# SSD's and mLSTM's output norms moved out of the stage behind RWKV into the scans, and five more products of zeros in each chunk of the scan

## The reference, cut to what matters

```python
def _group_norm(y, g, n_groups, center, eps=1e-5):
    yf = y.reshape(shp[:-1] + (n_groups, shp[-1] // n_groups))
    if center:
        yf = yf - jnp.mean(yf, axis=-1, keepdims=True)
    yf = yf * lax.rsqrt(jnp.mean(yf * yf, axis=-1, keepdims=True) + eps)
    return yf.reshape(shp) * g
# SSD:   _group_norm((y_f + y_b + d_skip * xs) * silu(z), norm_g, 2, center=False)
# RWKV:  _group_norm(o_f + o_b, norm_g, 4, center=True) * gate
# mLSTM: _group_norm(h_f + h_b, norm_g, 4, center=True) * sigmoid(o)
y = concat([y_ssd, y_rwkv, y_ml]) @ w_out;  x = x + g1 * y
```

## Time and profile before

| | us |
|---|---|
| median of 3 runs | 2280.27 |
| the runs | 2279.90, 2280.27, 2293.11 |
| the profiled execution | 2292.93 |
| its span, first to last instruction | 2291.2 |
| PE busy in it | 2125.0 (93%) |
| DVE, ACT, POOL busy | 838.0, 773.7, 742.2 |

### The profile page before, as it was taken

One profiled execution on the slowest core, in us unless ns is written; L12 is line 12 of the kernel. 1 busy time (PEld: TensorE's weight loads), 2 busy tenths in 40 slices (PEclk: granted clock), 3 DMA queues, 4 the chain that ended last, 5 costly groups with the idle time before them and its releaser, 6 DMA issues.

```text
span 2291.2 us, 46135 instructions
## 1 busy us (share of the span) xinstructions
PE 2125.0 (93%) x20582; PEld 1973.0 (86%) x20590; DVE 838.0 (37%) x1385; ACT 773.7 (34%) x1369; POOL 742.2 (32%) x543
## 2 busy tenths in 40 slices
PE   6999999889789999999979989988878899999999
PEld 6998766778589999999979987677868899999998
DVE  5845265464650111011148453655455311110112
ACT  4535453333242222121154364433232422222212
POOL 6432261224123333333322222522242233333331
PEclk8999998999899999999989999999998899999999
DMA  7553101000012222234326431010001122222222
GB/s 251 177 157 114 51 8 38 5 3 3 27 49 74 76 80 75 74 117 143 92 83 193 130 115 30 1 39 5 3 2 47 56 74 74 74 77 78 68 76 72
DMA packets 254305, 166.67 MB, mean 73 GB/s; under 512 B 23746, under 2 KB 228036, under 8 KB 254108
## 3 DMA queue, kind: packets, MB, share of 16 engines
q1 hardware_dynamic: 253881, 163.66, 24.1%
q10 hardware_dynamic: 227, 0.07, 0.0%
HBM read 159.59 MB, written 4.12 MB: 71 GB/s over the span
## 4 chain that ended last, share of the span: by engine, by line
PE 84%; DVE 6%; ACT 5%; issue 2%; POOL 1%; SPq 1%; DMA 0%; another core or an unknown queue 0%; DVEq 0%; ACTq 0%; POOLq 0%
PE PS L979 21%; PE PS L981 20%; PE PS L980 20%; PE PS L1373 5%; PE PS L937 2%; PE PS L1518 1%; PE PS L1391 1%; PE PS L1202 1%; PE PS L1439 1%; PE PS L1239 1%; PE PS L1045 1%; DVE U L2380 1%; PE PS L1253 1%; POOL ring_r L667 1%; PE PS L1472 1%
## 5 line engine op out<-in xcount | busy, mean ns | idle before, releaser
L979 PE MATMUL PS<-rwp_r,whi_r 128*128 128x320 f32 x2880 | 905.0, 314 | 40.4 <-POOL ring_r L667 16.6
L981 PE MATMUL PS<-rwp_r,ring_r 128*128 128x320 f32 x2880 | 897.2, 312 | 0.0
L667 POOL TENSOR_TENSOR ring_r<-ring,whi_r 128x1024 fp32r<-128x1024 f32 (+1 forms) x204 | 497.5, 2440 | 1116.4 <-ACT whi_r L1704 1116.4
L980 PE MATMUL PS<-arena_r,whi_r 128*128 128x320 f32 x2240 | 697.9, 312 | 0.0
L979 PEld LDWEIGHTS PS<-rwp_r,whi_r 128*128 128x128 f32 x2880 | 547.8, 190 | 55.9 <-issue 28.4
L981 PEld LDWEIGHTS PS<-rwp_r,ring_r 128*128 128x128 f32 x2880 | 547.3, 190 | 0.0
L980 PEld LDWEIGHTS PS<-arena_r,whi_r 128*128 128x128 f32 x2240 | 426.1, 190 | 0.0
L1704 ACT ACTIVATE whi_r<-ring 128x1024 fp32r<-128x1024 f32 (+1 forms) x204 | 211.4, 1039 | 542.0 <-PE PS L981 541.9
L980 PE MATMUL PS<-U_r,whi_r 128*128 128x320 f32 x960 | 298.2, 311 | 0.0
L2592 DVE TENSOR_TENSOR U<-arena,PS 128x640 f32<-128x640 f32 x44 | 36.1, 821 | 549.7 <-PE PS L981 549.7
L980 PEld LDWEIGHTS PS<-U_r,whi_r 128*128 128x128 f32 x960 | 181.7, 189 | 0.0
(11 more groups left out here) (385 smaller groups left out, 2660.2 us busy)
## 6 DMA issues: line engine op xcount, KB each, us to landing
ring<-in_ffn_w SPq DMA_DIRECT2D x120, 512.0 KB, 3.8
rwp<-in_ada_w SPq DMA_DIRECT2D x64, 512.0 KB, 4.8
ring<-in_w_in SPq DMA_DIRECT2D x50, 512.0 KB, 4.5
U<-in_ada_w SPq DMA_DIRECT2D x16, 512.0 KB, 8.1
ring<-in_w_out SPq DMA_DIRECT2D x16, 512.0 KB, 4.6
arena<-in_ada_w SPq DMA_DIRECT2D x16, 512.0 KB, 4.8
ring<-in_ffn_w SPq DMA_DIRECT2D x16, 384.0 KB, 3.3
out<-arena SPq DMA_DIRECT2D x5, 512.0 KB, 2.7
```

Of the source, the lines that this page charges most:

```text
L667: g.tensor_tensor(rings_r[:, slot_of[n], 0:size(n), :], slot(n)[:, 0:size(n), :], whis[:, q % 2, 0:size(n), :].bitcast(F32), ALU.subtract) ...
L979: mm(out, w[0][:, k, :], hi[:, cols], start=start, stop=False)
L980: mm(out, w[0][:, k, :], lo[:, cols], start=False, stop=False)
L981: return mm(out, w[1][:, k, :], hi[:, cols], start=False, stop=stop)
```

## The change

SSD and mLSTM no longer take part in the stage behind RWKV.

- **mLSTM**, in `normalise(c)`: DVE now adds the two directions, sums each head (a reduction), subtracts the mean, squares and sums again into `YN`: five more instructions per chunk. Three of them stand ahead of `ym_ready`, for which `mlstm_back` waits; all five stand ahead of the next chunk's `weights`. `mlstm_back` becomes two transposes instead of four products.
- **SSD**: POOL gates chunk by chunk (`gate(c)`), ACT squares (`y_squares`, two chunks behind, and the last two after the first decays), and PE sums the squares in RWKV's step 0 with 20 products of one column.
- ACT takes the square roots at the end of step 0, DVE the reciprocal in step 1, PE turns the 30 columns of `YN` in step 2, DVE copies them, and SP (`norm_rows`) writes them to DRAM and reads them back repeated over the partitions (a DMA of 128x1280 and two of 64x2x640). DVE waits for these inside step 2 and then scales SSD's and mLSTM's tiles; ACT's high and DVE's low parts follow in steps 3 and 4. The loads of `w_out` 2 and 3 wait until the rows are used.
- **The stage behind** holds RWKV's norm alone; its reciprocal is over 320 columns instead of twice 640, and the products of `w_out` for the six tiles that are ready stand between its steps.
- **Zeros**: one more product with zeros in each of the three groups of `e_rows`, one more in `w_rows(c+1, 0)` and one in `w_rows(c+1, 1)`: five per chunk, in four of the five chunks.

The core of the diff:

```diff
 # tensor: e_rows, the chunk loop, mlstm_back
-                            mm(PS[:, b, :], identb[:, :], NEG[:, P - 1:P].broadcast_to((P, 4 * P)), start=False,
-                               stop=True).then_inc(s["ec_mm"], 1)
+                            for n_ in range(2):
+                                ins = mm(PS[:, b, :], identb[:, :], NEG[:, P - 1:P].broadcast_to((P, 4 * P)),
+                                         start=False, stop=n_ == 1)
+                            ins.then_inc(s["ec_mm"], 1)
...
-                            w_rows(c + 1, 0, 2)
+                            w_rows(c + 1, 0, 3)
...
-                            w_rows(c + 1, 1)
+                            w_rows(c + 1, 1, 1)
...
-                            for d in range(2):
-                                ins = mm(PS[:, 6, f * P:(f + 1) * P], YM[:, d, f * P:(f + 1) * P], ident[:, :],
-                                         start=d == 0, stop=d == 1)
+                            ins = tr(PS[:, 6, f * P:(f + 1) * P], YM[:, 0, f * P:(f + 1) * P], ident[:, :])
...
 # tensor: RWKV
+                        if k == 0:
+                            pe.wait_ge(s["rw_tok"], at["rw_tok"] + 2)
+                            pe.wait_ge(s["ysq_ready"], at["ysq_ready"] + NC)
+                            for c in range(NC):
+                                for q in range(4):
+                                    n = NC * (q // 2) + c
+                                    ins = mm(PS[:, 0, n:n + 1], U[:, Z + q, ck(c)], ones[:, 0:1], start=q % 2 == 0,
+                                             stop=q % 2 == 1)
+                            ins.then_inc(s["yn_mm"], 1)
...
 # tensor: the stage behind
+                    for f in range(2):
+                        g_job(2 * f, [(BO[:, :], U[:, Z + f, :])]).then_inc(s["g_mm"], 1)
                     w01 = [split_block(Q_WOUT + m) for m in range(2)]
+                    out_rows(range(3))
+                    pe.wait_ge(s["g_src"], at["g_src"] + 1)
+                    for f in range(2):
+                        g_job(2 * f, [(BO[:, :], U[:, BT_ + f, :])]).then_inc(s["g_mm"], 1)
+                    out_rows(range(3, 4))
...
+                    out_rows(range(4, 6))
+                    pe.wait_ge(s["g_rec"], at["g_rec"] + 1)
...
+                    out_rows(range(6, 8))
 # scalar
+                            if i == 4 and c > 1:
+                                y_squares(c - 2)
...
+                            A(YN[:, 0:2 * NC], YN[:, 0:2 * NC], ACT.Sqrt, bias=eps[:, 2:3], scale=1.0 / 256)
...
 # vector: normalise
+                        v.tensor_tensor(YS, YM[:, 0], YM[:, 1], ALU.add).then_inc(s["dve_step"], 1)
+                        v.tensor_reduce(YMEAN, heads(YS, 4), AX.X, ALU.add).then_inc(s["dve_step"], 1)
+                        v.scalar_tensor_tensor(out=heads(YM[:, 0], 4), in0=wide(YMEAN, 64), scalar=-1.0 / 64,
+                                               in1=heads(YS, 4), op0=ALU.mult, op1=ALU.add).then_inc(s["ym_ready"], 1)
+                        v.tensor_tensor(YM[:, 1], YM[:, 0], YM[:, 0], ALU.mult).then_inc(s["dve_step"], 1)
+                        v.tensor_reduce(YN[:, 2 * NC + c::NC], heads(YM[:, 1], 4), AX.X, ALU.add).then_inc(
+                            s["dve_step"], 1)
...
 # vector: RWKV, step 4, where prep_scan stood, and step 2
+                            for f in range(2):
+                                v.tensor_tensor(U[:, MV + f, :], U[:, MV + f, :], U[:, MO + f, :],
+                                                ALU.mult).then_inc(s["y_done"], 1)
+                            for n in range(2):
+                                y_low(n)
...
+                            if l == 0 and k == 2:
+                                dve.wait_ge(s["yn_in"], at["yn_in"] + 16 * 4)
+                                ssd_scaled(range(2))
```

More of the change, by code:

```diff
@@ L150, in build @@
                   for l in range(DEPTH)]
+        yn_d = [nc.dram_tensor("yn%d" % l, (6, NC * P), F32, kind="Internal").ap() for l in range(DEPTH)]
         PS = ctx.enter_context(nc.psum_tensor("PS", [P, 8, 512], F32))
@@ L541, in _ @@
                             sp.wait_ge(s["yt_read"], at["yt_read"] + NC)
+                        if blk == (lay, "w_out", 2):
+                            norm_rows()
                         if blk == (lay, "w_out", RING):
@@ L796, in scans @@
                             skip(c)
+                            gate(c - 2)
+                        for c in range(NC - 2, NC):
+                            gate(c)
                     def chunk_keys(k):
@@ new lines, in _ @@
+                    ins.then_inc(s["g_mm"], 1)
+                    out_rows(range(4, 6))
+                    pe.wait_ge(s["g_rec"], at["g_rec"] + 1)
+                    for f in range(2):
+                        for hf in range(2):
+                            rows = slice(64 * hf + 32 * f, 64 * hf + 32 * f + 32)
+                            ins = mm(PS[:, 2 * f + hf, 0:HALF], SPREAD[rows, :], gtmp[rows, 3, 0:HALF], start=True,
+                                     stop=True)
+                        ins.then_inc(s["g_mm"], 1)
@@ L1887, in _ @@
                     decays(0)
+                    for c in range(NC - 2, NC):
+                        y_squares(c)
                     for k in range(NC):
@@ L1953, in _ @@
+                    act.wait_ge(s["g_mm"], at["g_mm"] + 5)
+                    A(gtmp[:, 3, 0:HALF], PS[:, 0, 0:HALF], ACT.Sqrt, bias=eps[:, 2:3], scale=1.0 / 64).then_inc(
+                        s["g_std"], 1)
+                    y_high(range(6, 8))
                     for k in range(KT):
@@ L2527, in centre @@
                             s["g_read"], 1)
-                    for n in range(2):
-                        centre(MV + n, 4 + 2 * n, 3 + n)
                     dve.wait_ge(s["g_read"], at["g_read"] + 2)
@@ L2565, in _ @@
-                    y_low(7)
+                        centre(BT_ + n, 2 * n, 3 + n)
+                    dve.wait_ge(s["g_std"], at["g_std"] + 1)
+                    v.reciprocal(gtmp[:, 3, 0:HALF], gtmp[:, 3, 0:HALF]).then_inc(s["g_rec"], 1)
+                    for f, gate in enumerate((LORA, MISC)):
+                        y_ = U[:, BT_ + f, :]
+                        dve.wait_ge(s["g_mm"], at["g_mm"] + 6 + f)
+                        v.scalar_tensor_tensor(out=pair(y_), in0=pair(y_), scalar=col(lay, "rwkv_norm_g", f),
+                                               in1=PS[:, 2 * f:2 * f + 2, 0:HALF], op0=ALU.mult,
+                                               op1=ALU.mult).then_inc(s["dve_step"], 1)
+                        dve.wait_ge(s["dve_step"], step())
+                        v.tensor_tensor(y_, y_, U[:, gate, :], ALU.mult).then_inc(s["y_done"], 1)
@@ L2567, in residual @@
+                    for n in range(6, 8):
+                        y_low(n)
                     def residual(b, m, row, sem):
```

203 lines of the change are left out of this document (114 added, 89 removed).

## The result

| us | before | after |
|---|---|---|
| median (4 runs each) | 2282.89 | 2315.24 |
| lowest, highest | 2279.90, 2293.11 | 2313.63, 2327.95 |
| span and mean clock of the profiled run | 2291.2, 0.967 | 2312.9, 0.956 |

The two medians are 32 us apart; the ratio on record is 1.011 with an interval of 1.007 to 1.016: slower by 25 us where 10 us less was forecast. 2315 is outside the range of 2254 to 2288. With six more runs (d2_after) the ratio is 1.011 again, 1.007 to 1.014. The kernel before scatters between 2278 and 2310 in the later runs, with medians of 2291 to 2293, so all that follows goes by ratios and by stages of the traces.

What follows compares the result with a forecast made beforehand. PE was taken as the bound, with 84% of the chain that ended last. Stage behind −21.7, scan +12.4, RWKV +4.2 gave −5.1 us a layer, −10.3 in all: 2280.3 to a median of 2270, range 2254 to 2288.

Steps and rivals of the forecast that it cites:

- the stage behind: Stage behind RWKV: first block's end 26.2 us after RWKV's last read instead of 47.9, a gain of 21.7 a layer.
- the scan: Scan: DVE's five sums delay y_ssd by 1.76 and zeros add 0.88 per transition; 12.4 us a layer with the last chunk.
- the one-column products: RWKV's step 0: 40 instructions at 0.111, 4.44 us in all, making L1391 start 2.6 us later.
- step 4: RWKV's step 4: four DVE instructions of 0.8 us make PE wait, +1.25 us, of at most 3.2.
- Both signs of being wrong: Stage behind RWKV gives back less than 21.7 us, or a scan chunk grows by more than 3.9.
- rival A: Scan: PE's waits let the clock fall, 6.2 us a stretch; one more per layer gives 2282, chance 0.12; more, 0.07.
- two or more per layer: Scan: at least two additional low-clock stretches in each layer, 2295 us and above; chance 0.07.
- Step 0 with the scan's end: Last scan chunk +1.84 us (ACT's square, later ym_ready, shorter turn back) and RWKV's step 0 +2.6.
- rival B: RWKV's step 2: the rows come late from DRAM and DVE waits, 6.4 us a layer, 2283; chance 0.04.
- rival D: Stage behind RWKV: gaps between pieces of w_out keep PE at clock 0.50, some 3 us a layer, 2276; chance 0.10.
- The table load: RWKV: one more ACT activation-table load of 1.28 us, hidden in ACT's idle 2.29, priced at nothing.

Runs made afterwards that it cites:

- d2_after: The changed kernel itself, unaltered, run again in a later session: median 2318.6 us, ratio 1.011 to the kernel before.
- c2_stage: Changed kernel with the stage behind RWKV reordered: nine unused products behind PE's wait for POOL, one tile instead of three ahead of the means; 2324.2 us, ratio 1.017.
- c3_step0: Changed kernel with the 20 one-column products moved out of RWKV's step 0, to ahead of and behind mlstm_back(4); 2320.7 us, ratio 1.014.
- e2_before_wide: Kernel before with 24 unused bf16 products of 512 columns added in RWKV's step 0; 2302.7 us, ratio 1.005.
- b1_zeros: Kernel before with only the five new products of zeros per chunk added; 2294.6 us, ratio 1.001.
- a3_nosums: Changed kernel with mLSTM's five DVE instructions left out in chunks 0 to 3 and made in chunk 4 alone; 2279.8 us, ratio 0.996.
- c1_late: Changed kernel without new zeros, DVE's five sums put between and behind the next chunk's weights, mLSTM turned back behind y_ssd(c, 0); 2280.1 us, ratio 0.996.
- d1_best: Changed kernel with c1_late's order, one-column products outside step 0 with wide ones between, stage behind reordered and filled, step 4's DVE work spread; 2250.4 us, ratio 0.983.

## Why the prediction was wrong

**The step that failed.** The sum takes every new wait, every new product and every handover at its own length, at full clock, and puts the low clock behind them at nothing. The runs showed it in four of its terms: up to 11.8 us a layer in the scan, 1.6 behind the one-column products, 1.45 in step 4 and 3.6 in the stage behind. Both signs of being wrong that I had named came: the stage behind gave back 18.3 and not 21.7, and a chunk grew by 5.6, more than 3.9.

**The scan.** The delays were right (sums 2.3 us, PE's wait 1.80, 9.2 a layer against 10.6). Wrong was the chance of rival A. I had a price for it (6.2 for the long stretch of before; here 3.2 a chunk) and its cause, and gave "two or more per layer" 0.07. The evidence I set against it was that layer 1's scan idles 3.2 us of 35 at full clock, a mean over many short waits. The change makes one of 1.8, and none of my rows of before shows a wait of that length in a scan at full clock. Layer 0 pays 11.8 us for that in four of the five profiles that have this scan and 3.9 in c2_stage, layer 1 between 1 (first profile) and 11.7 (c3_step0). That is the largest part of the miss.

I had also taken the row at 345 to 355 as agreeing that the clock falls on an inactive PE. It does not. The windows ahead of it, in the kernel before:

```profile
335.00:340.00 5.00, 5.00 (x68) 3.68 (x65) 2.30 (x5) 2.90 (x11) 0.00 (x0) 1.00 0.00 0
340.00:345.00 5.00, 4.75 (x22) 3.79 (x22) 4.96 (x6) 0.00 (x0) 4.29 (x3) 0.74 0.01 3
```

PE was all but always busy, and from 327 us to where the clock fell no wait was over 0.25 us. So the long wait brings the low clock on, as filling it and taking it away both show, and a scan can lose its clock without one. What sets that off stays open.

**RWKV.** Step 0 with the scan's end was forecast at +4.4 and came to +7.9 and +7.4. The products cost 5.19 for 40 instructions (0.13 each, 0.111 taken from the earlier trace rows), and behind them the clock is at half:

```profile
414.95 5.19 PE L1407 MATMUL PS<-ones,U 128*128 128x1 f32 x40
420.07 3.68 PE L1420 MATMUL PS<-arena 64*64 64x64 f32 x64
```

The same 64 take 2.08 at full clock in e2_before_wide. I had counted these products as work like other work. From step 0's first 64x256 product to step 4's the change costs 0.3 where the clock is whole, as forecast (142.1 at the least, against 141.8 in b1_zeros); that layer 0 took 4.5 more than before there and layer 1 5.0 less are low stretches of both kernels, which no run here explains. In step 4 DVE's four instructions were priced at +1.25 and brought +3.35:

```profile
1706.19 2.25 DVE L2569 TENSOR_TENSOR U<-U 128x640 f32<-128x640 f32 x2
1708.36 2.06 DVE L2510 TENSOR_TENSOR U_r<-U,rwp_r 128x640 fp32r<-128x640 f32 x2
...
1710.91 1.15 PE L1420 MATMUL PS<-arena 64*64 64x64 f32 x32 [1.74 <-DVE arena L2553]
...
1714.44 1.06 PE L1420 MATMUL PS<-arena 64*64 64x64 f32 x16
```

They took 4.3 us instead of 3.2 (POOL worked on the bonus at the same time; no run parts the two), PE comes to its product 1.8 later, and behind that wait 16 products take 1.06 instead of 0.63. Where the clock is whole behind it, as in a3_nosums's layer 1, this part takes 28.6: +1.9 is DVE's, 1.45 the clock's. I had taken the wait of a step with `prep_scan` for the whole price. The rows came in time: DVE waits for no DMA, so rival B is out.

**The stage behind.** Forecast 26.2, measured 29.6. Its steps:

```profile
1735.65 0.39 PE L1010 MATMUL PS<-rwp_r,whi_r 128*128 128x320 f32 x1 [2.32 <-POOL ring_r L694]
...
1737.05 0.47 PE L1011 MATMUL PS<-U_r,whi_r 128*128 128x320 f32 x1
...
1742.54 2.31 PE L1569 MATMUL PS<-U,BO 128*128 128x320 f32 x8
...
1747.97 2.15 DVE L2659 RECIPROCAL arena<-arena 128x320 f32<-128x320 f32 x1 [2.25 <-ACT arena L2014]
...
1756.05 0.41 PE L1010 MATMUL PS<-rwp_r,whi_r 128*128 128x320 f32 x1 [4.22 <-DVE U_r L2510]
...
1758.79 0.47 PE L1010 MATMUL PS<-rwp_r,whi_r 128*128 128x320 f32 x1
```

The blocks are whole 4.75 us after the start (4.1 forecast), the 36 products take 6.9 (5.2), from the means to the last wait's end 13.5 (14.2), from there to the first block's end 4.5 (2.6). The two that are longer by 1.7 and 1.9 have products of 0.27 us from start to start in them, from the fifth or sixth product behind waits of 2.32 and 4.22 on: rival D, at 3.6 against its price of 3, to which I gave 0.10 as if it excluded the forecast. It was no rival but a part of it, though not a certain one: in c1_late's layer 0 the 36 products behind a wait of 2.33 ran at 0.15 and the stage took 28.0. d1_best shows that the order and the filling had 7 us more to give: the means, which everything else waits for, stood behind 36 products that nobody waited for.

**Together.** The undisturbed scan, the scan's end with step 0, step 4 and the stage behind make 9.2 + 7.4 + 3.35 − 18.3 = +1.7 a layer where −5.1 was forecast: 14 us for two. The scans' low stretches are 13 us in the first profile and between 8 (c2_stage) and 23 (c3_step0) in others; the one in before's scan was 5.9. This does not add up to the whole miss. The first profile took 32 us more than the 2282.6 forecast on its footing. The table's stages give 21 of them (+10.5 where −10.3 was forecast). The other 11 lie outside: 4.9 ahead of layer 0's scan, 2.3 between layer 0's first block and layer 1's scan, 4.0 behind layer 1's first block. No run isolates these; over all profiles the start alone scatters by 6 us (312.6 to 318.6). The low clock is in all four terms that failed. I had weighed it in two of them, as A and D, and in the other two not at all.

The table load was rightly priced at nothing: up to step 4 the changed kernel loses 0.3 us where the clock is whole. The Trainium skill gives 2.66 us for a switch with its drain (ScalarE: Activation LUTs, What ACT_TABLE_LOAD costs). In the changed kernel's trace ACT's next instruction starts 1.30 us behind the start of the load, so the drain does not show:

```profile
453.73 1.28 ACT L2000 ACT_TABLE_LOAD   x1
455.03 0.30 ACT L2000 ACTIVATE YN<-YN,eps 128x10 f32<-128x10 f32 x1
```

## What to carry to other kernels

Before work is moved onto an engine that PE waits for, look at the longest single wait that this makes, not at PE's mean idle time, and count behind it PE's products at half clock; the same holds at every new gap, in one sum. Put the moved work behind what PE wants next, as c1_late does, and start the chain that others wait for before the independent products that are to cover it. If a wait stays, wide products of which nothing is kept can be cheaper than the wait alone (24 us here); the narrow ones tried gave back some 7.

## What I had not expected of the hardware

- Adding 56 products of which nothing is kept (7 in 8 places, 1.67 us each time) made the changed kernel 24 us faster, and leaving out 40 made it no faster (2321.3 against 2315 to 2319).
- PE at 5.00 us busy of 5 on fp32 products of one column had its clock fall to 0.64, and it was 0.50 behind them; on bf16 products of 512 columns, as long, it stayed at 1.00. The busy share in the records doesn't tell whether the clock will hold. The Trainium skill (TensorE: Matmul & The Clock Gate, What's actually happening) says that activity releases the slow state; in these rows PE is busy throughout and the slow state comes all the same.
- The low stretches depend on more than the place: the same wait costs layer 0 its clock in all four chunks in four profiles and in two of them in c2_stage, and layer 1 in one to four, from profile to profile. Some come with no wait at all. What decides it there stays open; so does how much of e2_before_wide's surplus is due to it.
